# Where expert fetches stand among the stages of a hybrid decoder layer, and who sums them

## What is computed

```python
h  = rmsnorm(x);  b, c, x_in, q_lat, kv_lat, k_rope, gate_c, gate_a = split(h @ w_in)
y_c = (b * conv3(c * x_in)) @ w_conv_out            # short convolution
y_a = attention(q_lat, kv_lat, k_rope) @ w_attn_out  # latent attention, 8 heads
x  = x + (sigmoid(gate_c) * y_c + sigmoid(gate_a) * y_a) @ w_mix_out
h  = rmsnorm(x)
s  = per head and side: (h @ w_peer_q) . sub_keys    # 8 heads, 2 sides, 128 keys
best 16 of each side, then best 16 of their sums -> expert numbers and softmax weights g
x  = x + sum over the 128 picks of  g * gelu(u[pick] . h) * v[pick]
```

## Time and profile before

| | us |
|---|---|
| median of 3 runs | 3855.89 |
| lowest, highest | 3852.59, 3856.81 |
| the profiled execution | 3849.86 |
| its span | 3848.0 |

### The profile page before, as it was taken

How to read it: one execution, slowest core, us unless ns; L and a number is a source line. 1 busy time by engine, 2 the same in 40 slices (tenths; PEclk the granted TensorE clock), 3 DMA queues, 4 the chain that set the end, 5 groups by cost and what they waited for, 6 DMA issues and landing times.

```text
span 3848.0 us, 35282 instructions
## 1 busy us (share of the span) xinstructions
PE 3180.5 (83%) x10224; PEld 1795.4 (47%) x10224; DVE 2629.8 (68%) x5829; ACT 1363.3 (35%) x3982; POOL 1089.7 (28%) x1252
## 2 busy tenths in 40 slices
PE   6797898867899898467778898889488989898877
PEld 4433686424455455134434454444244545676421
DVE  1354115987677779877677867789777677656774
ACT  1122202348612233255563222343244444222333
POOL 0000001333233333333333333334333233322342
PEclk9898699978999999788889998999788898665999
DMA  2112245999999998799999999999799899999999
GB/s 93 35 37 65 84 150 217 399 363 397 381 390 417 396 355 326 278 404 400 387 403 419 419 411 419 401 400 405 306 412 376 347 383 370 368 391 414 411 393 381
DMA packets 234016, 1289.23 MB, mean 335 GB/s; under 512 B 45467, under 2 KB 59867, under 8 KB 98340
## 3 DMA queue, kind: packets, MB, share of 16 engines
q0 software_dynamic: 152064, 1107.36, 71.0%
q1 hardware_dynamic: 80036, 175.28, 13.0%
q10 hardware_dynamic: 1728, 4.39, 0.3%
HBM read 1273.53 MB, written 13.40 MB: 334 GB/s over the span
## 4 chain that ended last, share of the span: by engine, by line
PE 35%; DMA 26%; DVE 18%; ACT 5%; issue 4%; POOL 1%; SPq 0%; DVEq 0%; POOLq 0%; ACTq 0%
DMA tl_uv<-in_uv,tl_idx 24%; PE tl_y L926 11%; PE tl_f L1175 8%; DVE tl_uv L1501 6%; DVE tl_acc L1482 3%; PE tl_f L1155 3%; PE tl_f L1203 3%; PE tl_f L987 2%; PE tl_f L1186 2%; PE tl_f L1099 1%; PE tl_f L1051 1%; POOL tl_uv L857 1%; DVE tl_eq L1601 1%; PE tl_f L1122 1%; ACT L1250 1%
## 5 line engine op out<-in xcount | busy, mean ns | idle before, releaser
L1501 DVE CUSTOM_DVE_ANT_0 tl_uv<-tl_uv,tl_h 128x1024 f32<-128x1024 f32 x1056 | 1270.8, 1216 | 539.9 <-DMA tl_uv<-in_uv,tl_idx 527.5
L857 POOL DMA_INDIRECT tl_uv<-in_uv,tl_idx x1056 | 1031.2, 977 | 1835.5 <-PE tl_y L926 1098.1
L926 PE MATMUL tl_y<-tl_uv,tl_diag 128*128 128x512 f32 (+1 forms) x2428 | 1293.0, 674 | 293.9 <-ACT tl_diag L1222 293.2
L926 PEld LDWEIGHTS tl_y<-tl_uv,tl_diag 128*128 128x128 f32 (+1 forms) x2428 | 478.9, 209 | 934.4 <-issue 466.6
L1250 ACT ACTIVATE tl_ge<-tl_a 128x1 f32<-128x1 f32 x1056 | 210.7, 199 | 1355.2 <-DVE tl_a L1501 1353.1
L1482 DVE SCALAR_TENSOR_TENSOR tl_acc<-tl_uv,tl_w,tl_acc 128x1024 f32<-128x1024 f32 x441 | 564.8, 1281 | 41.3 <-ACT tl_w L1234 41.3
L1234 ACT ACTIVATE tl_w<-tl_ge,tl_weight 128x1 f32<-128x1 f32 x1024 | 301.5, 294 | 33.4
L1175 PE MATMUL tl_f<-H,w_tail 128*128 128x384 f32 (+2 forms) x1024 | 280.0, 434 | 11.9 <-DMA w_tail<-in_w_merge 7.1
L1203 PE MATMUL tl_f<-H,w_tail 128*128 128x384 f32 (+2 forms) x1024 | 264.7, 414 | 9.3 <-DVE H L1803 9.1
L869 POOL TENSOR_TENSOR tl_cand<-tl_tv 128x48 f32<-128x48 f32 (+5 forms) x128 | 39.2, 335 | 816.6 <-DVE tl_ti L1533 620.5
L1222 ACT ACTIVATE tl_diag<-K,tl_w 128x128 f32<-128x128 f32 (+1 forms) x607 | 241.1, 397 | 34.2 <-PE tl_y L926 14.9
(11 more groups left out here) (227 smaller groups left out, 3026.1 us busy)
## 6 DMA issues: line engine op xcount, KB each, us to landing
w_tail<-in_w_merge SPq DMA_DIRECT2D x96, 512.0 KB, 7.8
w_tail<-in_w_peer SPq DMA_DIRECT2D x64, 576.0 KB, 7.9
w_tail<-in_w_conv SPq DMA_DIRECT2D x48, 512.0 KB, 7.8
tl_uv<-in_uv,tl_idx POOLq DMA_INDIRECT x1056, 11.4
w_tail<-in_w_mix SPq DMA_DIRECT2D x32, 512.0 KB, 7.8
X<-in_cache SPq DMA_DIRECT2D x48, 128.0 KB
X<-in_x SPq DMA_DIRECT2D x8, 536.0 KB, 6.9
o_y<-tl_acc ACTq DMA_DIRECT2D x8, 512.0 KB, 6.2
```

The lines of the kernel that those rows point to most:

```text
L857: pool.indirect_dma_start(UV[:, u % RING, :], None, d["uv"], bass.IndirectOffsetOnAxis(ap=which, axis=0)).then_inc(landed[u % RING], 16)
L926: mm = pe.matmul(Y[0:m, half * 512:(half + 1) * 512], DG[:, (pe_count[u] - 1) % DIAGS, 0:m], UV[:, u % RING, D + half * 512:D + (half + 1) ...
L1501: dve.tensor_tensor_reduce(UV[:, u % RING, 0:D], UV[:, u % RING, 0:D], HP[:], 1.0, 0.0, ALU.mult, ALU.add, A[:, t % 2, i:i + 1]).then_inc( ...
```

## The change

Three edits, all in the planner; no instruction of a stage is altered. The ticks of the three prompt chunks are given by a table, `LOAD`, with one value each for an attention item, a gate, a ranking step and the steps after ranking, and new constants for the others. `EDGE` for the ends of chunks 1 and 2 goes from 40 and 56 units past the chunk's start to 88 and 69, and `HEADS` of these two chunks gets one group more, at head 6. And `by_dve` gives VectorE seven units in eight rather than three in four from convolution to the end of mix.

```diff
--- before.py
+++ after.py
@@ -692,9 +692,10 @@
 
 
         DEC = 9 * NSEQ + 9
+        LOAD = [(8, 9, 16, 8), (11, 9, 22, 12), (18, 10, 26, 20)]
         PRE = [len(x) + 5 + NCV for x in items] + [DEC + NCV]
-        TICK = [[6 + 2 * PARTS[c][1]] * len(items[c]) + [8] * 5 + [8] * NCV
-                + [8, 8, 4, 4] * KD + [12] + [8] * KD + [16] + [16] * HC + [8] * 4 + [0] for c in range(NCH - 1)]
+        TICK = [[item] * len(items[c]) + [8] * 5 + [9] * NCV + [gate, gate, 5, 5] * KD + [12] + [9] * KD + [16]
+                + [rank] * HC + [rest] * 4 + [0] for c, (item, gate, rank, rest) in enumerate(LOAD)]
         TICK.append([12, 9, 9, 10, 10, 11, 11, 16, 11] * NSEQ + [4, 4, 4, 6, 6, 4, 6, 8, 8] + [6] * NCV
                     + [6, 6, 3, 3] * KD + [16] + [6] * KD + [16] + [12] * HC + [12] * 4 + [0])
         passed = [[0] + list(itertools.accumulate(x)) for x in TICK]
@@ -702,11 +703,11 @@
 
         LAG_ACT, LAG_DVE, LAG_POOL = 3, 6, 8
 
-        HEADS = [[1, 2, 4, PH]] * (NCH - 1) + [[PH]]
+        HEADS = [[1, 2, 4, PH]] + [[1, 2, 4, 6, PH]] * (NCH - 2) + [[PH]]
         group = lambda c, h: next(k for k, e in enumerate(HEADS[c]) if h < e)
         groups_to = lambda c, k: sum(len(x) for x in HEADS[:c]) + k
         weighed_at = lambda h: 2 * h + 5
-        EDGE = [56, begin[1] + 40, begin[2] + 56, begin[3]]
+        EDGE = [56, begin[1] + 88, begin[2] + 69, begin[3]]
 
         def due(c, i, lag, half=False):
             if c == 0:
@@ -728,7 +729,7 @@
                 if u < due(c, END, 0):
                     if u >= due(c, RANK, 0):
                         return u % 8 == 7
-                    return u % 4 != 0 if u >= due(c, -NCV, 0) else u % 2 == 1
+                    return u % 8 != 0 if u >= due(c, -NCV, 0) else u % 2 == 1
             return False
 
         pe_count = list(itertools.accumulate(0 if by_dve(u) else 1 for u in range(UNITS)))
```

## The result

The changed kernel takes 3898.93 us (median of 4 runs, 3890.14 to 3900.45) against 3855.88 (median of 4): ratio 1.0118, 95% interval 1.0101 to 1.0135. It is slower by 1.2%. Its profiled execution has a span of 3895.9 us, 47.9 more than the 3848.0 of before. I had forecast slower, by 18 us.

A forecast was written before the change was run, and what follows sets the result against it. Transfers, at about 400 GB/s, were taken to set the pace nearly everywhere, at 2.51 us a unit. The terms summed to +17, called +18: 3868 us on the profiled execution, 3874 as median, range 3825 to 3925.

The forecast's parts named there:

- Stop and go: Chunk 1 ranking: targets held at 256, 272, 288, 320 make four fetch bursts with pauses; +119 us, 3864 to 3905, chance 0.50.
- chunk 1's convolution to ranking: Chunk 1 before its ranking: 18 more units, transfers setting the pace, 323 us, +36 (bounds +31 and +45).
- Transfers bind, with less idle than before: I take 330, +33: Chunk 2's ranking with its end: 21 more units, 297 us growing to 330 (bounds +20 and +53).
- Chunk 2's attention: Chunk 2 attention until its convolution: 41 units fewer at 2.51 us each, -103 us (bound -110).
- convolution to projection: Chunk 2 from convolution to ranking: 17 units fewer, -43 us, VectorE staying at 90 sums.
- unchanged GB/s: Sign to look for: chunk 2's attention about 100 us shorter with its transfer rate the same.
- Decode: Decode stretch: two units fewer, -5 us.
- the 46 that the pauses cost beyond transfers: Chunk 1 ranking: +119 us for 29 units whose transfer costs 73.
- The faster one: Chunk 1's ranking takes about 300 us, its term +39, time 3794; faster overall mostly 3815 to 3848, chance 0.24.
- The clock's rival: Chunk 1 ranking bursts: TensorE's clock falls, a unit costing more than a transfer; 41 us, some 3915, chance 0.10.
- The early softmax group: Group of heads 4 to 6, done in a pause: costs nothing; without that cover 3 us each in chunks 1 and 2.

The follow-up runs named there:

- e11: The changed kernel with chunk 1's row of the tick table at (10, 8, 19, 36) in place of (11, 9, 22, 12): 3857.99 us, ratio 1.0009.
- e13: Edges, head groups and sums of e10, but the tick table of the kernel before: 3911.21 us, ratio 1.0136.
- e10: The changed kernel with EDGE[1] at begin[1]+64 in place of +88: 3841.75 us, ratio 0.9974.
- e4: The kernel before with seven sums in eight on VectorE and nothing else changed: 3854.70 us, ratio 1.0004.
- e2: The changed kernel with EDGE[1] back at begin[1]+40, all else kept: 3850.25 us, ratio 0.9990.
- e7: The kernel before with EDGE[1] at begin[1]+24 in place of +40: 3844.71 us, ratio 0.9980.
- e9: The kernel before with EDGE[1] at begin[1]+88, the changed head groups, and chunk 1 ticks of 21 per ranking step and 40 after: 3847.46 us, ratio 0.9986.
- e14: e10 with three sums in four on VectorE in place of seven in eight: 3844.81 us, ratio 0.9946.
- e15: The changed kernel with EDGE[1] at begin[1]+56 in place of +88: 3829.53 us, ratio 0.9910.
- e6: The changed kernel with HEADS of chunks 1 and 2 at [1, 2, 3, 4, 5, 6, PH]: 3898.06 us, ratio 1.0104.

## Why the prediction was right in sign and wrong in size

The account by stretch. Forecast terms are those of the prediction, measured lengths from the two profiled executions.

| stretch | before | after | measured | forecast |
|---|---|---|---|---|
| until chunk 1's convolution | 1056 | 1054 | -2 | -5 |
| to its first projection | 287 | 331 | +44 | +36 |
| its ranking | 261 | 379 | +118 | +119 |
| chunk 2 attention | 448 | 362 | -86 | -103 |
| to its first projection | 398 | 358 | -40 | -43 |
| its ranking | 307 | 359 | +52 | +33 |
| decode | 568 | 547 | -21 | -5 |
| the rest | 523 | 506 | -17 | -15 |
| sum | 3848 | 3896 | +48 | +17 |

*The mechanism.* Stop and go happened as worked out. The pauses between issues are 46.5, 25.0, 36.8 and 36.8 us; the last unit issued takes some 11 us to land, so transfers idled for about 35, 14, 26 and 26. The prediction had 35, 12, 25 and 25, and 380 us for the stretch. That holding causes it is shown by e11 (same edges, TensorE's target held for one step only, 41 us less) and e13 (smaller edge, held, 52 us over before; with the same edge and the change's ticks e10 is under before).

*The step that failed* is the sum over the stretches around it: the terms of chunk 1's convolution to ranking and of chunk 2, in which units were priced at 2.51 us and idle transfers were credited on top. Their sizes were wrong, not the path. "Transfers bind, with less idle than before: I take 330, +33" is the largest of them, 19 us off. Its base was read short as well: the 297 us began at 2461, 11 us after the first projection, and the 96 units were VectorE's count. By GpSimd's count that stretch went from 103 to 122 fetches; 19 x 2.51 is 48 of the measured 52. Its idle did not shrink (307 - 103 x 2.51 - 23 = 25 us before, 359 - 122 x 2.51 - 23 = 30 after), and why is my reading only: TensorE and VectorE, at 294 and 301 of 359 us, still wait for each other step by step. Chunk 2's attention gave back 86 of 103 us, its convolution to projection 40 of 43. The prediction wanted unchanged GB/s there; with 38 and 18 fetches fewer, and the attention's and the weights' loads the same, the rate fell from 392 to 376 and from 417 to 409. That the mixture of transfers does this isn't shown. Chunk 1's convolution to projection cost 8 us more than taken; 331 us is 108 fetches and the weights at the 410 GB/s it ran at, and e4 shows that relieving TensorE buys nothing there. Decode gave back 16 us more than its two units explain, in the other direction; why is open.

Put together, the terms up to the end of chunk 1's ranking were 10 us too low (160 measured, 150 forecast), and those after it gave back 21 us less than forecast (112, not 133). That is the 31 us between +17 and +48. Taken over the runs, the price is plainer. After chunk 1's ranking, the time left against the fetches left has a slope of 2.34 us a fetch (least squares over twelve kernels: before, the change and every experiment but e13; 707 to 768 fetches). Up to that point it is 2.23 us a fetch in the nine kernels whose target on TensorE waits at a limit for one step at most (before, e2, e4, e7, e9, e10, e11, e14, e15; 288 to 337 fetches). Both are estimates: single kernels lie up to 26 us off the first line and 15 us off the second, and the change lies beyond the end of the second. By them, moving 45 fetches ahead costs 100 us and gives back 105: nothing that can be told from zero. The line of the nine gives 1705 us for the change's 349 fetches, and it needed 1764. Those 60 us I put down to the holding: 60 - 5 against 48 measured. My own terms outside the pauses summed to a gain of 29 us (17 less the 46 that the pauses cost beyond transfers). The runs show no such gain, while the 46 lie between the 41 that e11 gave back with its shorter stops and these 60: it is the gain that was wrong, and not the pauses.

*The rivals.* The faster one, chunk 1 ranking as chunk 2 does, fell in the change. It came true in another shape once TensorE's target was held nowhere: e15 interleaves 20 more fetches with chunk 1's ranking in 29 us more, 1.45 us each. The Trainium skill, Perfetto Trace Analysis, section Optimization Strategy, which speaks for interleaving regimes, is borne out by e15; the change shows that more units assigned to a stretch aren't yet interleaved with it. The clock's rival did not come: in the first three bursts the granted clock was 0.80 to 0.86, in the last, after the 30 us wait, 0.75, and over the stretch 0.87 (0.90 before), with transfers at a share of 0.90 to 0.98 in all four. So its 41 us aren't in the 379. The Trainium skill's rule against gaps between bursts (TensorE: Matmul & The Clock Gate, Why this matters for your kernels) would have made it the likely one; here waits of up to 30 us went with a lower clock for part of a burst, not enough to make TensorE slower than transfers.

*The small costs.* The early softmax group cost nothing that shows; e6 has two more of them a chunk and the same time. The range, 3825 to 3925, held the result.

What stays open: why +56 beats +40 and +64, whose intervals lie above its own. e2, e10 and e15 ran on three chips, and the profiled executions can't tell: e15's took 3836.97 us and e10's 3835.65.

## What to carry to other kernels

When a schedule is written as targets against a readiness limit, work out each engine's target with its own lead against the limit: the leads that overlap two kinds of work vanish where all are cut to the same number, and at each such stop the fetches in flight run out and have to start again (in the change some 14 to 35 us of idle transfers each, an estimate from the pauses less 11 us). Where transfers bind on both sides, moving work between stages is worth nothing by itself, so don't credit idle time as recovered unless what caused it is removed. Finer groups did not help against the stops here; a target that rises more slowly through the ranking, or a smaller edge, did.

## What the runs showed that I had not expected

Cutting a 32-unit group in two left the time as it was (3898.06 against 3898.93 us), a pause of 36.8 us becoming two of 22.0 and 21.4. And pauses without fetched units did not all lower the granted clock alike. In the first pause TensorE did ranking matmuls (busy 31 of 31 us, clock 1.00) and then waited 12.4 us; the window of the burst, that wait included, has 0.80. Before the last burst it waited 30.0 us with no ranking matmul left, and this is TensorE's sums in that burst, same columns as the earlier trace rows:

```profile
1690.00:1764.00 74.00, 32.27 (x48) 10.50 (x48) 0.75 0.96 391
```

A sum of four records took 2.7 us there in the mean (32.27 us for 48), against 1.8 at full clock, with transfers at a share of 0.96 all the same.
